# The six quarters of the weight rings w_hi and w_lo set 32 bytes further apart in the on-chip memory

## The reference

```
x = x + concat(attention(q, k, v), groupnorm(retention(rq, rk, rv)) * silu(rg)) @ w_out   # proj = rmsnorm(x) @ w_in
x = x + (gelu(causal_dwconv(h @ w_up)) * (h @ w_gate)) @ w_down                            # h = rmsnorm(x), width 2816
x = x + (p @ w_ple) * sigmoid(rmsnorm(x) @ w_ple_gate);  x = rmsnorm(x)
x = x + (gate_a * (gated_delta_rule(...) @ w_proj_a) + gate_b * (sparse_attention(...) @ w_proj_b)) @ w_out_2
x = x + sum over the 2 chosen of 16 experts of weight * (silu(h @ w1) * (h @ w3)) @ w2     # router: top-1 group, top-2 experts
out = rmsnorm(x)
```

## Time and profile before

| | us |
|---|---|
| median of 3 runs | 848.62 (848.48 to 854.99) |
| the profiled execution | 846.92 |
| its span, first to last instruction | 845.1 |
| TensorE busy / weight loads busy | 819.4 / 734.4 |
| VectorE, ScalarE, GpSimd busy | 491.6, 466.4, 476.5 |
| granted TensorE clock | 0.996 of full |

### The profile page before, as it was taken

How to read it: one execution, slowest core, us unless ns; L and a number is a source line. 1 busy time by engine, 2 the same in 40 slices (tenths; PEclk the granted TensorE clock), 3 DMA queues, 4 the chain that set the end, 5 groups by cost and what they waited for, 6 DMA issues and landing times.

```text
span 845.1 us, 16275 instructions
## 1 busy us (share of the span) xinstructions
PE 819.4 (97%) x6273; PEld 734.4 (87%) x6273; DVE 491.6 (58%) x998; ACT 466.4 (55%) x735; POOL 476.5 (56%) x372
## 2 busy tenths in 40 slices
PE   8999999999999999899999999999999999999995
PEld 7998888999999998689988998999889888888883
DVE  3732434772321425763597735347477699999983
ACT  5434645645544655873547433235465578878763
POOL 5997585989999887787854443266877000000000
PEclk9999999999999999999999999999999999999998
DMA  8655244446555454535732221222536589999931
GB/s 319 222 204 195 100 150 161 165 168 221 208 199 199 158 193 147 188 131 156 227 116 100 101 93 60 102 102 100 200 147 223 226 334 369 352 385 351 375 123 50
DMA packets 24142, 160.98 MB, mean 190 GB/s; under 512 B 3201, under 2 KB 3729, under 8 KB 5393
## 3 DMA queue, kind: packets, MB, share of 16 engines
q1 hardware_dynamic: 21456, 154.67, 50.1%
q10 hardware_dynamic: 2624, 5.44, 2.0%
HBM read 157.62 MB, written 1.05 MB: 188 GB/s over the span
## 4 chain that ended last, share of the span: by engine, by line
PE 86%; DVE 8%; ACT 3%; issue 1%; DMA 1%; POOL 1%; SPq 0%; ACTq 0%; DVEq 0%
PE bank L1163 72%; PE bank L1698 3%; PE bank L1906 1%; PE bank L2023 1%; DMA raw<-weights_dram 1%; DVE work L2496 1%; DVE bank L2556 1%; POOL w_lo L594 1%; PE bank L1261 1%; ACT w_hi L635 1%; PE bank L1323 1%; PE bank L1309 1%; DVE best L2555 0%; PE bank L1727 0%; PE bank L1412 0%
## 5 line engine op out<-in xcount | busy, mean ns | idle before, releaser
L594 POOL TENSOR_TENSOR w_lo<-raw,w_hi 128x512 fp32r<-128x512 f32 x368 | 476.3, 1336 | 173.0 <-ACT w_hi L635 172.9
L1163 PE MATMUL bank<-h_hi,w_hi 128*128 128x256 f32 x864 | 247.5, 286 | 1.9 <-DVE h_lo L2123 1.4
L1163 PE MATMUL bank<-h_lo,w_hi 128*128 128x256 f32 x864 | 241.9, 280 | 0.0
L1163 PE MATMUL bank<-h_hi,w_lo 128*128 128x256 f32 x864 | 241.7, 280 | 0.0
L635 ACT ACTIVATE w_hi<-raw 128x1024 fp32r<-128x1024 f32 x184 | 187.9, 1058 | 81.2 <-DMA raw<-weights_dram 39.5
L1163 PEld LDWEIGHTS bank<-h_hi,w_hi 128*128 128x128 f32 x864 | 162.9, 189 | 6.3 <-DVE h_lo L2123 1.6
L1163 PEld LDWEIGHTS bank<-h_hi,w_lo 128*128 128x128 f32 x864 | 163.8, 190 | 0.0
L1163 PEld LDWEIGHTS bank<-h_lo,w_hi 128*128 128x128 f32 x864 | 162.7, 188 | 0.3
L1163 PE MATMUL bank<-w_hi,g_hi 128*128 128x512 f32 x208 | 81.7, 393 | 0.0
L1163 PE MATMUL bank<-w_hi,g_lo 128*128 128x512 f32 x208 | 81.1, 390 | 0.0
L1163 PE MATMUL bank<-w_lo,g_hi 128*128 128x512 f32 x208 | 81.1, 390 | 0.0
(11 more groups left out here) (407 smaller groups left out, 1345.7 us busy)
## 6 DMA issues: line engine op xcount, KB each, us to landing
raw<-weights_dram SPq DMA_DIRECT2D x119, 1024.0 KB, 4.8
spare<-weights_dram SPq DMA_DIRECT2D x18, 1024.0 KB, 6.6
tok<-weights_dram SPq DMA_DIRECT2D x9, 1024.0 KB, 5.8
x_sb<-x_dram SPq DMA_DIRECT2D x2, 512.0 KB, 4.4
work<-final_norm_dram ACTq DMA_DIRECT2D x2, 512.0 KB, 4.6
work<-work ACTq DMA_DIRECT2D x8, 128.0 KB, 5.7
work<-constants_dram ACTq DMA_DIRECT2D x1, 640.0 KB, 5.3
con<-constants_dram ACTq DMA_DIRECT2D x1, 520.0 KB, 3.7
```

Of the source, the lines that this page charges most:

```text
L594: ins = nc.gpsimd.tensor_tensor(w_lo[:, part], raw[:, part], w_hi[:, part].bitcast(F32), ALU.subtract)
L1163: ins = mm(dst, a, b, start=start and n == 0, stop=stop and n == 2, skip_group_check=True)
```

## The change

The quarters of w_hi and w_lo are set 1024 + 8 floats apart instead of 1024, so that each lies 32 bytes further on modulo 256 than the one before it. Ring positions 0 to 5 then begin at 128, 160, 192, 224, 0 and 32 modulo 256. The rings get 64 and 48 floats more and `h_before` goes, so that everything behind them lies 256 bytes higher: w_lo at 128, h at 64, g and the slots at 128 modulo 256 as before. raw keeps its layout. No instruction is added, removed or moved, and no shape changes.

```diff
+SHIFT = 8
-        w_hi = sb("w_hi", RING * QUARTER, F32R)
-        w_lo = sb("w_lo", RING * QUARTER, F32R)
-        sb("h_before", 48)
+        w_hi = sb("w_hi", RING * QUARTER + 64, F32R)
+        w_lo = sb("w_lo", RING * QUARTER + 48, F32R)
...
+        def staggered(q, i=0, n=1):
+
+            at = q % RING * (QUARTER + SHIFT) + i * (QUARTER // n)
+            return slice(at, at + QUARTER // n)
...
-                    ins = nc.gpsimd.tensor_tensor(w_lo[:, part], raw[:, part], w_hi[:, part].bitcast(F32), ALU.subtract)
+                    to = staggered(r, i, 2)
+                    ins = nc.gpsimd.tensor_tensor(w_lo[:, to], raw[:, part], w_hi[:, to].bitcast(F32), ALU.subtract)
...
-                nc.scalar.activation(w_hi[:, ring(q)], raw[:, ring(q)], ACT.Copy).then_inc(sem("hi_done"), 1)
+                nc.scalar.activation(w_hi[:, staggered(q)], raw[:, ring(q)], ACT.Copy).then_inc(sem("hi_done"), 1)
...
-                nc.scalar.activation(w_hi[:, ring(n)], slot_quarter(i), ACT.Copy).then_inc(sem("slot_hi_done"), 1)
+                nc.scalar.activation(w_hi[:, staggered(n)], slot_quarter(i), ACT.Copy).then_inc(sem("slot_hi_done"), 1)
...
-                return w_hi[:, ring(q)], w_lo[:, ring(q)]
+                return w_hi[:, staggered(q)], w_lo[:, staggered(q)]
...
-                V.tensor_tensor(w_lo[:, ring(n)], slot_quarter(i), w_hi[:, ring(n)].bitcast(F32), ALU.subtract)\
+                V.tensor_tensor(w_lo[:, staggered(n)], slot_quarter(i), w_hi[:, staggered(n)].bitcast(F32), ALU.subtract)\
```

## The result

| | us | against the kernel before |
|---|---|---|
| before, median of 10 runs | 848.65 | |
| after, median of 10 runs | 856.16 (854.79 to 870.24) | 1.0087, 95% interval 1.0071 to 1.0104 |
| after once more (`after_again`), beside 24 runs of before | 856.72 | 1.0106, interval 1.0080 to 1.0131 |

The time lies within the range, 839 to 860 us, but I had forecast -0.3 us, and the loss is 7.5 us and clear of the interval. The first profile of the changed kernel is a run of 870.24 us with a stall of VectorE; none of its other nine runs is above 858 us. The stall is told of at the end. The profile of `after_again`, 856.72 us with a span of 854.9, is the one to set beside the rows of before.

A forecast was written before the change was run, and what follows sets the result against it. The prediction took TensorE's number of matmuls times their pace as the bound. Its terms, -0.6 + 1.2 - 0.3 - 0.6 = -0.3 us, moved the median from 848.62 to about 848.3 us; range 839 to 860 us.

The forecast's parts named there:

- Reading the bound: Over most of the kernel, time is the number of matmuls times the distance between starts; TensorE busy 819.4 of 845.1 us.
- the rule of a TensorE that waits for no one: Trainium skill's claim that only VectorE and GpSimd contend for SBUF, making the change worth 0; not leaned on.
- Part 1, features with h: 2160 feature matmuls with h moving, weights loaded: 115.7 ns for 116, -0.6 us.
- The bounds: For features with h: -5.6 us if all at 113.4 ns, +8.6 us if all at 120.0; extreme -17 us.
- Part 2, weights moving against g, slots and p: 900 matmuls with weights moving: 228 ns for 226.7, +1.2 us; bounds 0 (or -10.5) and +6.8 us.
- the factor 5/6: Share of each kind of quarter taken as touched, since ring position 0 stays at 128 and the other five move.
- Part 3, against h: 320 matmuls with weights moving, h loaded: 228 ns for 228.9, -0.3 us; bounds -0.7 and +1.7 us.
- Part 4, g features: 160 matmuls with g moving, weights loaded: 116 ns for 120, -0.6 us; bounds -1.1 us and 0.
- Parts 5 and 6: Ring filling by ScalarE, GpSimd and VectorE, costed at nothing; HBM loads, SyncE's queue and semaphores unchanged in number and order.
- 120 ns everywhere: Rival: features with h at the other residues run at g's 120.0 ns, weights moving at 228.9; +10.6, 859 us; chance 0.22.
- The quick pace everywhere: Rival: 32-byte steps at quarter starts throw the feed-forward stage out of its slow phase; -7.4, 841 us; chance 0.17.
- The whole excess goes: Rival: opposite places free TensorE's two reads of each other, features towards 108 ns until GpSimd limits; 827 us; chance 0.07.

The follow-up runs named there:

- experiment 5: Kernel before with all of w 32, 64, 192 or 224 bytes on, h and g unmoved: 859.95, 856.29 (one run), 865.58 (one run), 859.12 us.
- run 7: Kernel before with ring position 0 160 bytes further on, only in the first blocks and the feed-forward stage: 846.21 us, 0.9966.
- runs 6: Kernel before with ring position 0 160 bytes further on up to the last stage, the other positions at 128 modulo 256: 847.42 us, 0.9983.
- `uniform_64`: Kernel before with w_hi and w_lo 64 bytes further on, all quarters alike: one run had VectorE's stall, the other took 856.29 us.
- `uniform_192`: Kernel before with w_hi and w_lo 192 bytes further on, all quarters alike: one run had VectorE's stall, the other took 865.58 us.
- `raw_only`: Kernel before with the halves of raw staggered by 64 bytes, w, h, g and slots as before modulo 256: 1.0064, and 1.0113 when repeated.

## Why the prediction was wrong

The step that failed is the choice of the paces for the residues not yet seen: 115.7 ns for features and 228 ns for the passes that move weights, both taken as lying among the paces that the kernel before showed. The runs showed 118.1 ns (mean of the unbroken feature quarters with h; 116.7 before) and 232 ns (mean distance of starts against g and the slots; 227 and 228 before).

**Reading the bound** held: the time is the number of matmuls times their pace, and the pace hangs on addresses modulo 256. That the rule of a TensorE that waits for no one could not be leaned on held as well: all weights 32 bytes off cost 1.3% (`uniform_32`).

**Part 1, features with h** (forecast -0.6 us, measured +2.9). It failed at the choice of 115.7 ns out of the earlier trace rows. The small projections load 24 columns, and what they do at mixed residues does not carry over to blocks of 128: full blocks at distances of 96 to 224 run at 117 to 120 ns (the table of experiment 5). The bounds held the truth. The loss did not come where I would have looked either. In the feed-forward stage features were at the slow 117.8 ns already and the mix cost them 0.04 us in eight quarters; it was the stretches at the quick pace, like the earlier trace rows, that lost: the first eight quarters took 0.6 us longer. That such a stretch had been quick was in part luck, as run 7 shows.

**Part 2, weights moving against g, slots and p** (forecast +1.2 us, measured +4.7). The larger miss, and of the same kind: I took a value between the two known paces, 228 ns, though the earlier trace rows showed 234. At distances of 32 to 160 these passes run at 229 to 234 ns. That no other residue would do better than 226.7 was said, and was right. That the sixth at ring position 0 would stay as it was, as the factor 5/6 has it, was wrong: 0.45 us of the loss lies there in the slot stage alone.

**Part 3, against h** (-0.3 us forecast; measured +0.8 without the quarter at half clock). Distance 64 had looked poor at 228.9; the others are poorer.

**Part 4, g features** (-0.6 forecast, -0.25 measured): right in sign.

**Parts 5 and 6** held: no engine that fills the rings changed its time, and TensorE waited for GpSimd 1.1 us in all, 1.3 before.

**The rivals.** "120 ns everywhere", 859 us, with 0.22, came nearest; its reason, that departing from the lowest pace can only cost, was the right one, and full blocks at the new distances run at 117 to 120 ns. Its price for the passes that move weights, 2.2 ns (+2.0 us), was too low against +4.7, and its price for the features, +8.6 us, too high against +2.9; the two misses partly cancel. Its sign that decides, a mean h pace of 119.7 ns or more, did not come. The quick pace everywhere did not come with this stagger, but its idea, that a step at a quarter's start can throw TensorE out of the slow phase, is what runs 6 and 7 show at distance 64 in unbroken stretches. "The whole excess goes" found nothing: no distance was under 113 and 227 ns. The formula that it took from the Trainium skill, "TensorE: Matmul & The Clock Gate", section "Back-to-back issue gap", stands there for a matmul by itself and not for a stream in which each has a load; no run here comes down to it with float32r.

What stays open: why the pace depends on the distance between TensorE's two operands, what a quarter takes over from the one before it, and why distance 64 knows two paces. That the two reads disturb each other is argued, not shown. The experiments give the table, not the mechanism.

## What to carry to other kernels

Where a chain of matmuls is unbroken, read the pace from starts, form by form, and compare it with columns over clock; 7 to 21 ns per matmul were to be seen here before the change, and weights 32 bytes off cost 1.3% of the kernel. Choose addresses by the distance between the loaded and the moving operand modulo 256 bytes (here 64 for 256 columns of float32r moving, 0 for 512), for each kind of pass by its number of matmuls, and keep neighbouring blocks at one residue unless a run shows that mixing pays. A value for an unseen case is not the mean of the seen ones when those were read at the best places; take the row with full-size blocks, and where there is none, give the bad side more weight.

## What the runs showed that I had not expected

**Duration is not pace.** The mean duration of the second h pass was 280 ns before and is 280 after, while the pace of the feature quarters without a wait rose by 1.4 ns. My conversion with a fixed 164 ns happened to give about the right mean before (116 for 116.7), and would have shown no change after. With 512 columns the durations did show the loss (390 became 394 to 395), though not its size: the pace rose by 4 to 5 ns in the mean.

**One instruction of VectorE can be held up by GpSimd for 20 us.** In the first profile of the changed kernel one TENSOR_SCALAR of VectorE over 256 columns in SBUF does not end while GpSimd runs 17 subtractions back to back. The timeline of VectorE (start us, us for all eight, idle before them):

```profile
24.61 21.99 DVE L2202 TENSOR_SCALAR work<-work 128x256 f32<-128x256 f32 x8 [10.12 <-DMA row<-dt_bias_dram]
```

The stretch, with the busy time of PE, PEld, DVE, ACT and POOL and the granted clock:

```profile
24.70:45.00 20.30, 10.73 (x92) 10.52 (x90) 20.30 (x1) 7.25 (x8) 20.30 (x17) 0.84 0.67 238
```

And of the waits, TensorE's on VectorE:

```profile
PE bank L1169 <- DVE work L2137: 12.4, 1, 12.4
```

The eight instructions take 21.99 us. The first lasts 20.58 us and ends 0.15 us after the last of the 17; the other seven take 0.28 us each. In the profile before the same eight took 6.35 us: four of them lasted 1.38 or 1.39 us beside subtractions of some 1.35 us, so there the two engines took turns. TensorE waited 12.4 us for what VectorE does next, and from 38.5 to 52.1 us it was busy for 4.2 us and its clock was at half. `uniform_64` and `uniform_192` had the same in their profiles (22.46 and 22.53 us for the eight; 5 to 10 us in the other ten profiles). The Trainium skill, "SBUF — State Buffer", section "SBUF: two separate sides", says that GpSimd and a VectorE instruction that needs the port pair they share take it as an exclusive lock for a whole instruction; the trace agrees, and the same side had it, as far as can be told from the times, 17 times in a row. Why the two engines took turns in ten profiles and not in three stays open. The three profiled runs with it lie 14 to 16 us above the other runs of the same kernels; whether other long runs have it too was not profiled.

**The clock can fall at a gap that was always there.** In `after_again`, around a thinning of TensorE's work in the middle of the kernel (us, PE busy, PEld, DVE, ACT, POOL, clock):

```profile
354.20:360.80 6.60, 3.35 (x19) 2.54 (x18) 4.62 (x14) 5.08 (x13) 3.21 (x3) 1.00 0.31 132
360.90:364.10 3.20, 3.20 (x9) 2.50 (x8) 3.13 (x11) 2.01 (x4) 0.00 (x0) 0.50 0.94 325
```

One quarter took 4.42 us there for 2.83 before. The same kernel can do either: `raw_only`, and then `raw_only_2`, which is the same kernel again, at the same place:

```profile
350.50:356.80 6.30, 2.93 (x17) 2.17 (x16) 4.32 (x14) 5.02 (x13) 2.96 (x3) 1.00 0.30 126
357.00:360.20 3.20, 3.20 (x9) 2.50 (x8) 3.13 (x11) 2.00 (x5) 0.00 (x0) 0.50 0.91 323
...
350.30:356.60 6.30, 3.24 (x18) 2.37 (x16) 4.33 (x13) 4.36 (x11) 3.63 (x3) 1.00 0.39 160
356.80:360.00 3.20, 3.13 (x14) 2.62 (x15) 3.13 (x9) 2.02 (x6) 0.00 (x0) 1.00 0.76 266
```

TensorE was busy about half of the time before it in all three; in two of them the 3.2 us behind it ran at 1.2 GHz, in the third at 2.4 GHz. So 1.6 us of difference between two profiles of such kernels can be this alone, and the 9.7 us between the two profiles of before and after here are 8.1 us of paces and 1.6 of it.
